# Two MLPs by one level of Strassen's algorithm: seven block products for eight

## The chip, the cores and the metric

One core of a Trainium2 chip runs the kernel. The metric is the device time of one execution in microseconds; of three runs of the kernel before the median was 3708.84 us (3703.24 to 3708.95).

TensorE multiplies: in this kernel a matmul holds a weight tile of 128x128, streams 512 columns past it and adds into a bank of 512 columns in PSUM; the part that changes uses eight banks. VectorE and ScalarE read PSUM and do everything elementwise, GpSimd works on SBUF, and SyncE (SP) issues DMAs. Each engine runs its own queue in order; they wait for each other by semaphores.

## The reference

The model works on x of 1024 tokens by 1024 channels. Two layers come first, an attention layer and a recurrent one, each followed by an MLP; then a norm and two mixed layers. All in fp32. The part that changes is the MLP:

```
def sqrelu_mlp(h, w1, w2):
    return jnp.square(jax.nn.relu(h @ w1)) @ w2
...
        x = x + sqrelu_mlp(rmsnorm(x, mlp_norm_g[layer]), mlp_w1[layer], mlp_w2[layer])
```

w1 is 1024x4096, w2 is 4096x1024. Behind the first MLP comes the recurrent layer, which starts with a norm of x; behind the second a norm and the mixed layers.

## The kernel before

All activations lie transposed: channels on partitions in eight tiles of 128, the 1024 tokens along the columns. An fp32 product is made of three: each operand is split into a high part, rounded to the fp32r that TensorE takes, and a low part, the rest, and high x high, high x low and low x high are summed.

`trunk` (L648) holds the attention's output projection (W_O), MLP 0, the recurrent layer (R_X, R_Y, R_O) and MLP 1. All weights come as panels of 128 output channels, 160 of them, through one loop on four queues:

- SP loads a panel of 512 KB into one of two slots as soon as the slot's last one was split (L151).
- GpSimd makes the high part (L711) and the low part (L713) of a panel, when TensorE is done with the slot's panel before.
- TensorE takes a panel in `product` (L198): for each of 8 chunks of input channels the three parts, for each part both halves of the tokens, so two neighbouring matmuls write two different banks (L208). 8 x 3 x 2 = 48 matmuls of 512 columns. Two panels have four banks, `pn.acc`; another four, `aux`, are for sums.
- VectorE and ScalarE empty them.

An MLP is done in four groups of 1024 hidden channels: eight panels of w1, then eight of w2. In the first kind (`mlp` of VectorE, L1002 to L1016) VectorE multiplies the relu by rstd, the norm's factor per token (L1008), ScalarE squares it (L873) and makes the high part (L875), VectorE the low part (L1011), while TensorE is at the next panel. In the second kind VectorE adds the panel to x (`add`, L977). The last panel of a group is the only one whose tile the next panel needs, as its last chunk.

Ahead of an MLP and behind it x is normed: ScalarE scales each finished tile (L859) and squares it (L861), VectorE makes the low part (L982) and sums the squares into one accumulator (L988), and TensorE sums that over the partitions (`total`, L766 to L772) before the last chunk of the next panel. ScalarE takes the root (L865), VectorE the reciprocal (L1000). Behind MLP 1 the squares are summed twice, plain and by the next norm's gain (L988, L1140).

Before the trunk's first panel TensorE runs filler matmuls (`keep_busy`, L521).

Of the kernel before, what the change touches and what calls it, by code (L numbers as in the profile page):

```python
# [2 lines left out]

# [15 lines left out]
P = 128  # L19
D = 1024  # L20
# [99 lines left out]
class Panels:  # L120
# [77 lines left out]
    def product(self, pe, u, turn, h_hi, h_lo, before_chunk=None, order=None):  # L198
# [4 lines left out]
        for k in order:  # L203
            if before_chunk:
                before_chunk(k)
            for part, (w, h) in enumerate(((self.hi, h_hi), (self.hi, h_lo), (self.lo, h_hi))):
                for s in range(2):
                    last = pe.matmul(self.acc[:, u, s * HALF:(s + 1) * HALF], w[:, u, k, :],  # L208
                                     h[:, k, s * HALF:(s + 1) * HALF],
                                     start=(k == order[0] and part == 0), stop=(k == order[-1] and part == 2))  # L210
        last.then_inc(self.sems[f"panel_done{u}"], 1)
# [272 lines left out]

class Model:
# [162 lines left out]
    def trunk(self, oT, held):  # L648
# [13 lines left out]
        with stage(nc, "tk", names) as (sems, sb, ps):  # L662
            a_lo = sb("a_lo", [P, DK, S], F32R)
            a_hi = sb("a_hi", [P, DK, S], F32R)
            with nc.sbuf_tensor("tk_xb", [P, DK, S], F32) as xb:
                pass
            b_lo = sb("b_lo", [P, DK, S], F32R)
            b_hi = sb("b_hi", [P, DK, S], F32R)
            with nc.sbuf_tensor("tk_xb_lo", [P, 2, S], F32R) as xb_lo:
                pass  # L670
            sq = sb("sq", [P, 2, S])
# [18 lines left out]
            with nc.Block() as block:  # L690
                @block.sync
                def _(sync):
                    for p in range(2, MLP[0]):
                        u = p % 2
                        sync.wait_ge(sems[f"w_split{u}"], p // 2 + 1)
                        sync.dma_start(pn.raw[:, u, W_O_AHEAD:DK, :].rearrange("p k n -> p (k n)"),
                                       self.ins["w_trunk"][p, :, W_O_AHEAD * P:]).then_inc(sems[f"w_landed{u}"], 16)
                    pn.load(sync, MLP[0] // 2)

                @block.gpsimd  # L700
                def _(pool):
# [5 lines left out]
                    def weights(turn, u, at=0):  # L707
# [4 lines left out]
                        pool.wait_ge(sems[f"w_hi{u}"], turn + 1)  # L712
                        pool.tensor_tensor(pn.lo[:, u, at:, :], pn.raw[:, u, at:, :], pn.hi[:, u, at:, :].bitcast(F32),  # L713
# [42 lines left out]
                    with pool.Fori(R_O // 2, 80) as i:  # L756
                        for u in range(2):
                            weights(i, u)

                @block.tensor  # L760
                def _(pe):
                    def ready(s):

                        return lambda k: pe.wait_ge(sems["x_lo"], DK * s + k + 1)

                    def total(s):  # L766

# [6 lines left out]
                    def first(s):  # L774

                        def before(k):
                            if k == DK - 1:
                                total(s)
                            ready(s)(k)

                        return before

                    def mlp(m, base, s):
                        hid = lambda g: (lambda k: pe.wait_ge(sems["hid_lo"], 32 * m + 8 * g + k + 1))
                        pn.product(pe, 0, base // 2, *A, first(s))
                        pn.product(pe, 1, base // 2, *A)
                        with pe.Fori(1, 4) as i:
                            for u in range(2):
                                pn.product(pe, u, base // 2 + i, *A)
                        with pe.Fori(0, 4) as i:  # L790
                            for u in range(2):
                                pn.product(pe, u, base // 2 + 4 + i, *B, hid(0))
                        with pe.Fori(1, FG) as g:
                            with pe.Fori(0, 4) as i:
                                for u in range(2):
                                    pn.product(pe, u, 8 * g + i + base // 2, *A)
                            with pe.Fori(0, 4) as i:
                                for u in range(2):
                                    pn.product(pe, u, 8 * g + i + (base // 2 + 4), *B, hid(g))
# [27 lines left out]
                    mlp(0, MLP[0], 0)  # L827
                    linear(R_X, first(1), 1)
# [2295 lines left out]
```

## Time and profile before

| | |
|---|---|
| median of 3 runs | 3708.84 us |
| the profiled execution's own time | 3708.65 us |
| its span, first to last instruction | 3706.9 us |
| granted TensorE clock, mean | 0.983 |
| TensorE busy | 3556.1 us, 96% |
| VectorE busy | 1665.9 us, 45% |
| ScalarE busy | 1096.2 us, 30% |
| GpSimd busy | 1198.2 us, 32% |

Busy time is the union of an engine's instructions; shares are of the span. In a row of the profile PE is TensorE, PEld its weight loads, DVE VectorE, ACT ScalarE and POOL GpSimd; L208 is line 208 of the kernel. The matmuls overlap in the records, so the distance of their starts is what one costs.

### The profile page before, as it was taken

The numbers are of one execution on the slowest core, as the hardware profiler recorded it, in microseconds if no ns is written. First come the engines' busy times: TensorE is split into PE (matmuls) and PEld (weight loads), VectorE is DVE, ScalarE is ACT, GpSimd is POOL, SyncE is SP. The second block draws the span as 40 slices with busy tenths as digits, with TensorE's granted clock in tenths as the row PEclk, the third lists the DMA queues.
The fourth block names the chain that finished last, engine by engine and source line by source line (L and its number), as shares of the span: only waits on it lengthen the run. The fifth ranks groups of instructions, "written<-read, shape, count | busy, mean of one in ns | idle before, by whom it ended". The sixth has DMA issues, their size and how long they took to land. (4 is left out here: it accounts for less than half of the span.)

```text
span 3706.9 us, 44331 instructions
## 1 busy us (share of the span) xinstructions
PE 3556.1 (96%) x17794; PEld 2812.5 (76%) x17794; DVE 1665.9 (45%) x1935; ACT 1096.2 (30%) x1665; POOL 1198.2 (32%) x695
## 2 busy tenths in 40 slices
PE   7999999999999999999999999899988999998898
PEld 6777777888888888788888888787645678765567
DVE  5666766312121259642121113555746542275566
ACT  2355453201010116521010101214435411253551
POOL 2455541333333337532333332222212122321214
PEclk9999999999999999999999999999999999999999
DMA  4243341111111121211111111122124121211423
GB/s 164 91 139 136 108 154 68 51 51 46 51 45 51 58 84 49 88 46 51 45 51 45 51 45 51 40 108 85 35 63 125 63 102 40 78 42 44 127 78 110
DMA packets 84159, 274.56 MB, mean 74 GB/s; under 512 B 9872, under 2 KB 11824, under 8 KB 84016
## 3 DMA queue, kind: packets, MB, share of 16 engines
q1 hardware_dynamic: 60720, 206.52, 16.3%
q10 hardware_dynamic: 16384, 40.90, 3.3%
q0 software_dynamic: 6912, 25.17, 2.0%
q8 instruction: 97, 1.59, 0.2%
q14 instruction: 46, 0.38, 0.0%
HBM read 220.39 MB, written 47.97 MB: 72 GB/s over the span
## 5 line engine op out<-in xcount | busy, mean ns | idle before, releaser
L711 POOL CAST held_hi<-held_raw 128x1024 fp32r<-128x1024 f32 (+1 forms) x158 | 174.1, 1102 | 1062.4 <-PE tk_acc L208 548.0
L208 PE MATMUL tk_acc<-tk_a_hi,held_hi 128*128 128x512 f32 x1280 | 396.4, 391 | 6.6 <-POOL held_lo L713 5.8
L208 PE MATMUL tk_acc<-tk_a_lo,held_hi 128*128 128x512 f32 x1280 | 394.7, 390 | 0.0
L208 PE MATMUL tk_acc<-tk_a_hi,held_lo 128*128 128x512 f32 x1280 | 394.6, 389 | 0.0
L873 ACT ACTIVATE tk_sq<-tk_r 128x1024 f32<-128x1024 f32 x64 | 67.9, 1061 | 1067.0 <-DVE tk_r L1008 1067.0
L713 POOL TENSOR_TENSOR held_lo<-held_raw,held_hi 128x1024 fp32r<-128x1024 f32 (+1 forms) x158 | 378.3, 2395 | 12.7
L208 PE MATMUL tk_acc<-tk_b_hi,held_hi 128*128 128x512 f32 x1200 | 369.5, 389 | 0.0
L208 PE MATMUL tk_acc<-tk_b_hi,held_lo 128*128 128x512 f32 x1200 | 369.5, 389 | 0.0
L208 PE MATMUL tk_acc<-tk_b_lo,held_hi 128*128 128x512 f32 x1200 | 369.4, 389 | 0.0
L977 DVE TENSOR_TENSOR xT<-tk_acc,xT 128x1024 f32<-128x1024 f32 x80 | 97.9, 1224 | 568.0 <-PE tk_acc L208 567.6
L208 PEld LDWEIGHTS tk_acc<-tk_a_hi,held_hi 128*128 128x128 f32 x1280 | 240.3, 188 | 58.9 <-POOL held_lo L713 7.9
L208 PEld LDWEIGHTS tk_acc<-tk_a_lo,held_hi 128*128 128x128 f32 x1280 | 240.8, 188 | 50.2
L208 PEld LDWEIGHTS tk_acc<-tk_a_hi,held_lo 128*128 128x128 f32 x1280 | 240.5, 188 | 50.1
L208 PEld LDWEIGHTS tk_acc<-tk_b_hi,held_lo 128*128 128x128 f32 x1200 | 225.2, 188 | 46.8
L208 PEld LDWEIGHTS tk_acc<-tk_b_lo,held_hi 128*128 128x128 f32 x1200 | 225.2, 188 | 46.7
L208 PEld LDWEIGHTS tk_acc<-tk_b_hi,held_hi 128*128 128x128 f32 x1200 | 225.2, 188 | 46.7
L1008 DVE SCALAR_TENSOR_TENSOR tk_r<-tk_acc,tk_rstd 128x1024 f32<-128x1024 f32 x64 | 78.4, 1224 | 393.4 <-PE tk_acc L208 393.2
L1961 PE MATMUL ma_sc<-xT 104*128 104x512 f32 (+5 forms) x384 | 157.0, 520 | 7.9 <-DMA xT<-mkpe_dram 5.2
L2513 POOL TENSOR_TENSOR da_mod_acc<-da_mod_acc,da_w_mod 128x1024 f32<-128x1024 f32 x42 | 115.6, 2753 | 124.0 <-ACT da_w_mod L2896 124.0
L2064 DVE TENSOR_REDUCE ma_st<-ma_sc 128x1 f32<-128x128 f32 (+7 forms) x128 | 96.7, 756 | 121.3 <-PE ma_sc L1961 120.6
L1011 DVE TENSOR_TENSOR tk_b_lo<-tk_sq,tk_b_hi 128x1024 fp32r<-128x1024 f32 x64 | 78.8, 1231 | 141.5 <-ACT tk_b_hi L875 141.5
L2205 ACT COPY ma_pts<-ma_pt 128x128 f32<-128x128 f32 (+7 forms) x128 | 81.7, 638 | 115.2 <-PE ma_pt L1973 114.5
(421 smaller groups left out, 6940.0 us busy)
## 6 DMA issues: line engine op xcount, KB each, us to landing
held_raw<-in_w_trunk SPq DMA_DIRECT2D x154, 512.0 KB, 3.1
da_w_mod<-in_ada_w POOLq DMA_DIRECT2D x48, 512.0 KB, 4.1
pj_w_raw<-in_w_in SPq DMA_DIRECT2D x44, 512.0 KB, 3.2
held_raw<-in_w_qkv SPq DMA_DIRECT2D x24, 512.0 KB, 3.7
ma_w_raw<-in_w_out SPq DMA_DIRECT2D x24, 512.0 KB, 3.2
x_dram<-xT ACTq DMA_DIRECT2D x16, 512.0 KB, 2.6
xT<-x_dram SPq DMA_DIRECT2D x16, 512.0 KB, 7.2
xT<-in_xT SPq DMA_DIRECT2D x13, 512.0 KB, 9.2
```

Of the source, the lines that this page charges most:

```text
L208: last = pe.matmul(self.acc[:, u, s * HALF:(s + 1) * HALF], w[:, u, k, :], h[:, k, s * HALF:(s + 1) * HALF], start=(k == order[0] and part ...
L711: pool.tensor_copy(pn.hi[:, u, at:, :], pn.raw[:, u, at:, :]).then_inc(sems[f"w_hi{u}"], 1)
L713: pool.tensor_tensor(pn.lo[:, u, at:, :], pn.raw[:, u, at:, :], pn.hi[:, u, at:, :].bitcast(F32), ALU.subtract).then_inc(sems[f"w_split{u} ...
L873: act.activation(sq[:, u, :], rr, ACT.Square).then_inc(sems["sq"], 1)
L977: dve.tensor_tensor(self.xT[:, n, :], pn.acc[:, p % 2, :], self.xT[:, n, :], ALU.add)\
L1008: dve.scalar_tensor_tensor(rr, pn.acc[:, u, :], 0.0, rstd[:, :], ALU.max, ALU.mult)\
L1011: dve.tensor_tensor(b_lo[:, n, :], sq[:, u, :], b_hi[:, n, :].bitcast(F32), ALU.subtract)\
L1961: last = pe.matmul(dst[:, part, :], q[0:rows, u % 2, m, b * P:(b + 1) * P], k[0:rows, u % 2, m, part * w:(part + 1) * w], start=True, stop ...
L2064: dve.tensor_reduce(st[:, t % 4, 1, m:m + 1], score(m, parts, w), axis=AXXY, op=ALU.max, negate=True).then_inc(sems["neg"], 1)
L2205: act.copy(pts[:, m, 0:n], pt[:, 0:n]).then_inc(sems["pts"], 1)
L2513: pool.tensor_tensor(mod_acc[:, j % 2, :], mod_acc[:, j % 2, :], w_mod[:, n % 2, :], ALU.add).then_inc(sems["mod_added"], 1)
```

## The change

A phase is a 1024x1024 block of weights times an operand of 1024 channels by 1024 tokens: four groups of an up and a down phase in each MLP, 16 in all (`ph`). Weights, operand and result are cut in two each way. Strassen's algorithm in Winograd's form makes the result's four blocks of seven products M1 to M7 of 512x512x512 blocks (before: eight), with sums of weight blocks on the left, of operand blocks on the right, and of products behind. They come in the order M1, M2, M4, M5, M6, M3, M7. A product is four units `p`, one for each tile of 128 output channels, and a unit is 12 matmuls into one bank: all four chunks high x high, then high x low, then low x high. Two units make a half-unit step `d` (14 a phase), which is the step in which weights are prepared: 128x1024 of a left operand.

- M1, M6 and M7 add up in the four banks of `pn.acc`; M2, M4, M5 and M3 in the four of `aux`. ScalarE copies M1's banks into `aux`, and M2 adds onto the copy; so each bank of `aux` is written in full by a matmul before the trunk.
- SP loads a phase's weights in eight blocks, the next phase's behind the sums that free them. GpSimd does nothing for the MLPs. ScalarE makes the high parts (`s_high`, `t_high`), VectorE the low parts (`s_low`, `t_low`) and all sums (`s_sum`, `t1_sum` to `t4_sum`), for the step or product after the one on TensorE. Weight parts have two slots by `d`, operand parts two by product.
- In an up phase VectorE relus M2's banks as it takes them, ScalarE takes M4, M5 and M6 to SBUF, VectorE adds M3 and M7 to these (two of 512 columns for each of M7's tiles), relus them (512 columns behind M3 in the last two steps, whole tiles behind M7 in the next phase's first step) and ScalarE squares them. VectorE takes all but M1 of a down phase and adds them to x.
- The panels of the other stages keep `product`; they are 32 now, and no loop is left in the MLPs. GpSimd waits for M7's units before it writes the low parts of R_X's first two panels, which share memory with the weight lows.
- Ahead of an MLP `a`, the operand in fp32, takes the place of its two parts; the sum of squares stands on TensorE behind M1's third unit; rstd's reciprocal comes in four quarters. Behind it tiles 0 to 3 of x are done with M3, tiles 4 to 7 with M7; `low_step` and `last` scale, split and square them.

The core of the diff, with twelve or more columns of indentation taken off:

```diff
+def left(d):
+    return [raw(11, d % 2), raw(12, d % 2), raw(22, d % 2), raw(22, d % 2), raw(22, d % 2), raw(22, d % 2),
+            raw(21, d % 2)][d % 14 // 2]
+def right(f, h):
+    ph, j = divmod(f, 7)
+    if j in (M1, M2, M3):
+        return operand(ph, *{M1: (0, 0), M2: (1, 0), M3: (1, 1)}[j], h)
+    if j == M6:
+        return tiles((hid_t2 if ph % 2 else a_t2)[:, h, :])
+    if j == M5 and ph % 2:
+        return tiles(t1[h])
+    return ts[:, f % 2, 1, 2 * h:2 * h + 2, :]
...
+def load_next(m):
+    for ph in range(8 * m, 8 * m + 7):
+        for at, q, d in ((12, 0, 10), (12, 1, 11), (22, 0, 10), (11, 0, 12), (22, 1, 11), (11, 1, 13),
+                         (21, 0, 12), (21, 1, 13)):
+            if at in (12, 11):
+                sync.wait_ge(sems["s_sum"], 8 * ph + d - 5)
+            else:
+                sync.wait_ge(sems["s_lo"], 14 * ph + d + 1)
+            load_block(ph + 1, at, q)
...
+    elif j == M2:
+        pe.wait_ge(sems["read_act"], wg.a_at[ph, M1, p])
...
+def product(ph, j):
+    f = 7 * ph + j
+    for p in range(4):
+        d = 2 * f + p // 2
+        if p % 2 == 0:
+            pe.wait_ge(sems["s_hi"], d + 1)
+        bank_ready(ph, j, p)
+        bank = bank_a(p) if j in (M1, M6, M7) else bank_b(p)
+        for part, (w, y) in enumerate(((s_hi, 0), (s_hi, 1), (s_lo, 0))):
+            if p % 2 == 0 and part == 2:
+                pe.wait_ge(sems["s_lo"], d + 1)
+            for k in range(4):
+                if p == 0 and k % 2 == 0 and part < 2:
+                    pe.wait_ge(sems[("t_hi", "t_lo")[part]], 2 * f + k // 2 + 1)
+                at = p % 2 * HALF + k * P
+                last = pe.matmul(bank, w[:, d % 2, at:at + P], tr[:, f % 2, y, k, :],
+                                 start=(j in (M1, M4, M5) and k == 0 and part == 0),
+                                 stop=(k == 3 and part == 2), skip_group_check=True)
+        last.then_inc(sems["unit"], 1)
+        if ph % 8 == 0 and j == M1 and p == 2:
+            total(ph // 4, 1)
...
-self.keep_busy(pe, aux[:, 1, 0:P], 28)
+self.keep_busy(pe, aux[:, 1, 0:P], 14)
+for p in range(4):
+    pe.matmul(bank_b(p), self.ident[:, :], self.xT[:, 0, 0:HALF], start=True, stop=True)
...
-mlp(0, MLP[0], 0)
-linear(R_X, first(1), 1)
+mlp(0)
+pe.wait_ge(sems["read_dve"], wg.d_at[7, M7, 1])
+linear(R_X, first_of_branch, 1)
+pe.wait_ge(sems["read_dve"], wg.d_at[7, M7, 3])
...
+    if d == 112:
+        act.wait_ge(sems["ai_done"], DK)
+    elif d >= 2:
+        act.wait_ge(sems["unit"], 2 * d - 2)
+    act.copy(tiles(s_hi[:, d % 2, :]), left(d)).then_inc(sems["s_hi"], 1)
...
+    src, dst = {M1: (bank_a(p), bank_b(p)), M4: (bank_b(p), piece(hid, p + 4, 0)),
+                M5: (bank_b(p), piece(hid, p + 4, 1)), M6: (bank_a(p), piece(hid, p, 1))}[j]
+    act.copy(dst, src).then_inc(sems["read_act"], 1)
...
+def mlp(m, finish_step):
+    for ph in range(8 * m, 8 * m + 8):
+        for d in range(14):
+            at = 14 * ph + d
+            f = at // 2
+            if not (ph % 8 == 0 and d == 0 or ph % 8 == 7 and d == 13):
+                s_high(at + 1)
+            if ph % 2 and d < 2:
+                for p in (2 * d, 2 * d + 1):
+                    square_tile(ph - 1, p)
+            if f + 1 < 56 * m + 56:
+                t_high(f + 1, d % 2)
+            prev, jj = divmod(at - 1, 14)
+            jj, q = jj // 2, (at - 1) % 2
+            if prev == ph and (jj == M1 or ph % 2 == 0 and jj in (M4, M5, M6)):
+                if ph % 8 == 0 and jj == M1 and q == 1:
+                    root(2 * m, 1)
+                    act.wait_ge(sems["root"], 2 * m + 1)
+                for p in (2 * q, 2 * q + 1):
+                    take(ph, jj, p)
...
+def park(step):
+    for kind, n in (((scaled, 0), (scaled, 1)), ((scaled, 2), (scaled, 3), (square, 0), (square, 1)),
+                    ((scaled, 4), (scaled, 5), (square, 2), (scaled, 6), (scaled, 7), (square, 3),
+                     (square, 4), (square, 5), (square, 6), (square, 7)))[step]:
+        kind(n)
...
+def s_low(d):
+    dve.wait_ge(sems["s_hi"], d + 1)
+    dve.tensor_tensor(tiles(s_lo[:, d % 2, :]), left(d), tiles(s_hi[:, d % 2, :].bitcast(F32)),
+                      ALU.subtract).then_inc(sems["s_lo"], 1)
...
+def t2_sum(ph, h):
+    hidden(ph, 1, h)
+    made(ph, f"t1_{h}")
+    difference(tiles(hid_t2[:, h, :]), operand(ph, 1, 1, h), tiles(t1[h]))
+def t4_sum(ph, h):
+    made(ph if ph % 2 else ph // 8 * 8, f"t2_{h}")
+    difference(slot(ph, M4, h), tiles((hid_t2 if ph % 2 else a_t2)[:, h, :]), operand(ph, 1, 0, h))
...
+        elif j == M7:
+            dve.tensor_tensor(x(1, 0), bank, x(1, 0), ALU.add)
+            last = dve.tensor_tensor(x(1, 1), bank, x(1, 1), ALU.add)
...
+def relu_tile(ph, p):
+    dve.wait_ge(sems["read_dve"], wg.d_at[ph, M7, p])
+    dve.scalar_tensor_tensor(hid[:, p + 4, :], hid[:, p + 4, :], 0.0, rstd[:, :], ALU.max, ALU.mult)\
+        .then_inc(sems["relu"], 1)
...
+def down(ph, finish_step):
+    end = ph % 8 == 7
+    for d in range(14):
+        at, f, h = 14 * ph + d, 7 * ph + d // 2, d % 2
+        if d == 0:
+            for p in range(2):
+                relu_tile(ph - 1, p)
+            s_low(at + 1)
+            for p in (2, 3):
+                take(ph - 1, M7, p)
+            t_low(f + 1, h)
+            for p in (2, 3):
+                relu_tile(ph - 1, p)
+            continue
+        due = [(ph, (d - 1) // 2, p) for p in ((0, 1) if d % 2 else (2, 3)) if d > 2]
+        if due:
+            take(*due[0])
+        if d == 1:
+            t1_sum(ph, 0)
+        elif d in (2, 3):
+            t2_sum(ph, h)
+        elif d in (10, 11):
+            t3_sum(ph, h)
+        if not end or d < 13:
+            s_low(at + 1)
+        if d == 1:
+            t1_sum(ph, 1)
+        elif d in (2, 3):
+            t4_sum(ph, h)
+        elif 4 <= d <= 11:
+            s_sum(at + 2)
...
+        if not end or d < 12:
+            t_low(f + 1, h)
+        if due:
+            take(*due[1])
+        if end and d >= 12:
+            finish_step(d - 12)
+    if end:
+        for p in (2, 3):
+            take(ph, M7, p)
+            finish_step(p)
...
+def low_step(step):
+    low = lambda n: split_low(n, self.col("mix_g", DK + n))
+    for kind, n in (((low, 0), (low, 1)), ((low, 2), (low, 3)), ((low, 4), (low, 5)),
+                    ((low, 6), (low, 7)) + tuple((partial(add_hidden_square, 1), n) for n in range(DK)))[step]:
+        kind(n)
...
+def last(step):
+    for n in ((0, 1), (2, 3), (4, 5), (6, 7))[step]:
+        add_hidden_square(3, n)
+        dve.wait_ge(sems["g_sq"], n + 1)
+        dve.wait_ge(sems["g_acc"], n + 1)
+        dve.tensor_tensor(rstd[:, :], rstd[:, :], a[:, n, :], ALU.add).then_inc(sems["g_acc"], 1)
```

## Rows read from the trace of the kernel before

**Rows 1.** The page's first part: busy us, share of the span, instructions.
```profile
PE 3556.1 (96%) x17794; PEld 2812.5 (76%) x17794; DVE 1665.9 (45%) x1935; ACT 1096.2 (30%) x1665; POOL 1198.2 (32%) x695
```

**Rows 2.** Windows, both MLPs: us; busy PE, PEld, DVE, ACT, POOL; clock; DMA share, GB/s.
```profile
651.00:1349.00 698.00, 698.00 (x3076) 577.29 (x3077) 155.26 (x116) 85.68 (x81) 220.96 (x128) 1.00 0.15 54
1672.00:2362.00 690.00, 690.00 (x3043) 570.68 (x3042) 148.50 (x113) 83.46 (x79) 213.22 (x124) 1.00 0.13 46
```

**Rows 3.** Timeline, VectorE amid an MLP: start, us, line, operation [idle before, releaser].
```profile
1023.05 1.23 DVE L1008 SCALAR_TENSOR_TENSOR tk_r<-tk_acc,tk_rstd 128x1024 f32<-128x1024 f32 x1 [6.21 <-PE tk_acc L208]
...
1026.49 1.23 DVE L1011 TENSOR_TENSOR tk_b_lo<-tk_sq,tk_b_hi 128x1024 fp32r<-128x1024 f32 x1 [2.21 <-ACT tk_b_hi L875]
1033.93 1.23 DVE L1008 SCALAR_TENSOR_TENSOR tk_r<-tk_acc,tk_rstd 128x1024 f32<-128x1024 f32 x1 [6.22 <-PE tk_acc L208]
```

**Rows 4.** Timeline, TensorE in the last mixed layer's output projection (two of 384).
```profile
3640.22 0.39 PE L2020 MATMUL ma_sc<-ma_hi,ma_w_hi 128*128 128x512 f32 x1
3640.44 0.39 PE L2020 MATMUL ma_sc<-ma_lo,ma_w_hi 128*128 128x512 f32 x1
```

**Rows 5.** Timeline, VectorE where its instructions follow closely.
```profile
401.89 0.67 DVE L2758 SCALAR_TENSOR_TENSOR xT<-da_x,xT 128x512 f32<-128x512 f32 x1
402.49 0.67 DVE L2759 SCALAR_TENSOR_TENSOR xT<-da_x,xT 128x512 f32<-128x512 f32 x1
...
610.46 3.50 DVE L1023 TENSOR_TENSOR tk_b_lo<-oT,tk_b_hi 128x1024 fp32r<-128x1024 f32 x3 [6.29 <-ACT tk_b_hi L880]
```

**Rows 6.** Groups by line and shape: busy us, mean ns; idle before, releasers.
```profile
L873 ACT ACTIVATE tk_sq<-tk_r 128x1024 f32<-128x1024 f32 x64 | 67.9, 1061 | 1067.0 <-DVE tk_r L1008 1067.0
...
L1636 DVE RECIPROCAL pj_rt<-pj_rt 128x256 f32<-128x256 f32 x32 | 56.1, 1753 | 17.9 <-ACT pj_rt L1484 17.1
...
L988 DVE TENSOR_TENSOR acc<-acc,tk_r 128x1024 f32<-128x1024 f32 x32 | 49.7, 1552 | 9.3 <-ACT tk_r L861 9.0
...
L2885 ACT COPY da_pts<-da_pt 128x512 f32<-128x512 f32 x48 | 28.2, 587 | 141.0 <-PE da_pt L2656 141.0
```

**Rows 7.** Timeline, VectorE at the start of the first mixed layer.
```profile
2387.25 1.28 DVE L422 SCALAR_TENSOR_TENSOR pj_ab<-xT,pj_h_g,pj_aux 128x1024 f32<-128x1024 f32 x1
2388.45 1.28 DVE L434 SCALAR_TENSOR_TENSOR m_h_lo<-pj_ab,mod,m_h_hi 128x1024 fp32r<-128x1024 f32 x1
2389.84 1.28 DVE L422 SCALAR_TENSOR_TENSOR pj_ab<-xT,pj_h_g,pj_aux 128x1024 f32<-128x1024 f32 x1
```

**Rows 8.** Timeline, the end of the first MLP.
```profile
1354.04 1.21 DVE L988 TENSOR_TENSOR acc<-acc,tk_r 128x1024 f32<-128x1024 f32 x1
...
1358.70 1.88 PE L770 MATMUL tk_aux<-acc,ones 128*128 128x512 f32 x4
```

**Rows 9.** Timeline, VectorE and GpSimd at the start of the first MLP.
```profile
652.98 2.40 POOL L713 TENSOR_TENSOR held_lo<-held_raw,held_hi 128x1024 fp32r<-128x1024 f32 x1
...
653.16 3.30 DVE L988 TENSOR_TENSOR acc<-acc,tk_r 128x1024 f32<-128x1024 f32 x1
...
657.59 1.23 DVE L988 TENSOR_TENSOR acc<-acc,tk_r 128x1024 f32<-128x1024 f32 x1
```

**Rows 10.** Windows, in the recurrent layer where TensorE stands.
```profile
1537.00:1542.00 5.00, 0.18 (x1) 0.00 (x0) 3.79 (x3) 1.06 (x1) 4.92 (x2) 1.00 0.00 0
1542.00:1545.00 3.00, 2.77 (x7) 2.21 (x8) 1.89 (x2) 1.04 (x1) 2.92 (x3) 0.58 0.52 173
```

**Rows 11.** Timeline, VectorE at the end of the second MLP.
```profile
2361.92 1.22 DVE L977 TENSOR_TENSOR xT<-tk_acc,xT 128x1024 f32<-128x1024 f32 x1 [6.17 <-PE tk_acc L208]
...
2365.41 1.22 DVE L1140 TENSOR_TENSOR tk_rstd<-tk_rstd,tk_sq 128x1024 f32<-128x1024 f32 x1
```

**Rows 12.** Timeline, TensorE at the start of the trunk.
```profile
608.38 9.19 PE L521 MATMUL tk_aux<-ones,ident 128*128 128x128 f32 x56 [3.11 <-PEq L79]
```

**Rows 13.** The page's DMA issues: count, KB each, median us to landing.
```profile
held_raw<-in_w_trunk SPq DMA_DIRECT2D x154, 512.0 KB, 3.1
```

**Rows 14.** Window in a mixed layer, columns as in rows 2.
```profile
2640.00:2710.00 70.00, 64.97 (x303) 43.54 (x303) 38.03 (x52) 24.16 (x40) 19.13 (x16) 1.00 0.07 25
```

More of the change, by code:

```diff
@@ L196, in credit, with product @@
             pe.sem_inc(self.sems[f"panel_done{u}"], 1)
-    def product(self, pe, u, turn, h_hi, h_lo, before_chunk=None, order=None):
+    def product(self, pe, u, turn, h_hi, h_lo, before_chunk=None, order=None, behind=None):
         pe.wait_ge(self.sems[f"w_split{u}"], turn + 2)
@@ L210, in product @@
                                      start=(k == order[0] and part == 0), stop=(k == order[-1] and part == 2))
+            if behind and k == behind[0]:
+                last.then_inc(self.sems[behind[1]], 1)
         last.then_inc(self.sems[f"panel_done{u}"], 1)
@@ L692, in _, with load_block @@
                 def _(sync):
[L693 to L698, printed above, removed]
+                    def load_block(ph, at, q):
+                        b, rows = at % 10 - 1, MLP[ph // 8] + 8 * (ph % 8) + 2 * q + 4 * (at // 10 - 1)
+                        sync.dma_start(raw(at, q), w_trunk[rows:rows + 2, :, b * HALF:(b + 1) * HALF]
+                                       .rearrange("a p m -> p a m")).then_inc(sems[f"raw{at}_{q}"], 16)
@@ L783, in mlp, with first_of_branch @@
[L783 to L799, printed above, removed]
+                    def first_of_branch(k):
+                        if k == DK - 1:
+                            total(1, 0)
+                        pe.wait_ge(sems["x_lo"], k + 1)
@@ L801, in blocks, with mlp @@
+                    def mlp(m):
+                        for ph in range(8 * m, 8 * m + 8):
+                            for j in range(7):
+                                product(ph, j)
                     def blocks(n):
@@ new lines, in into_mlp @@
+                    def into_mlp(m, base):
+                        for n in range(DK):
+                            if n == (6, DK - 1)[m]:
+                                if m:
+                                    s_low(112)
+                                for h in range(2):
+                                    t_low(56 * m, h)
+                            if n == DK - 1 and not m:
+                                s_low(0)
+                            add(base + n, n)
+                            if n == DK - 1:
+                                s_low(112 * m + 1)
+                            evacuated(dve, base + n)
+                            if n:
+                                add_square(2 * m, n - 1)
+                        add_square(2 * m, DK - 1)
@@ new lines, in difference, with hidden, a_t2_first @@
+                    def difference(out, x, y, op=ALU.subtract):
+                        dve.tensor_tensor(out, x, y, op).then_inc(sems["t_sum"], 1)
+                    def hidden(ph, block, h):
+                        if ph % 2:
+                            dve.wait_ge(sems["hid"], wg.squares(ph, block, h))
+                    def a_t2_first(ph, h):
+                        dve.wait_ge(sems["a_new"], ph + DK)
+                        difference(tiles(a_t2[:, h, :]), operand(ph, 1, 1, h), operand(ph, 0, 1, h))
@@ L1019, in _, with mlp @@
+                    def mlp(m, finish_step):
+                        for ph in range(8 * m, 8 * m + 8, 2):
+                            up(ph)
+                            down(ph + 1, finish_step)
                     for u in range(2):
```

414 lines of the change are left out of this document (304 added, 110 removed).

## The prediction

> **What bounds the kernel now.** I began with the page's busy times and then asked for stretches of the two MLPs. TensorE is busy 96% of the span [rows 1], and in the MLPs all of the time: 698.00 of 698 us in the first, 690.00 of 690 in the second, at granted clock 1.00, the 2.4 GHz level; VectorE works 155 and 149 us there, ScalarE 86 and 83, GpSimd 221 and 213 [rows 2]. The timeline shows the beat: VectorE's relus come every 10.88 us and each has stood 6.2 us for TensorE, never the reverse [rows 3]. A panel has 48 matmuls, so one costs 10.88 / 48 = 0.2267 us. All 128 panels of the MLPs take 1392.6 us. Only fewer matmuls, or a slower beat, can move the time here.
>
> **The change, part by part.** The sum is made against the profiled execution's own 3708.65 us (span 3706.9 and 1.75 around it), 0.2 us below the median of the three timed runs.
>
> *Removed: one panel in eight.* A phase (one 1024x1024 weight block of one MLP, 16 in all) had 8 panels of 48 matmuls; it gets 7 products of 4 units of 12, as many per product as a panel had. 16 x 10.88 = **-174.1 us**, if a matmul keeps its price. Before, neighbours alternate between two banks; now 12 in a row fill one bank, and no two share a weight tile. The output projection of the mixed layers already writes 24 in a row into one bank, with a weight tile of its own each: starts 0.22 to 0.23 us apart [rows 4]. I take no change.
>
> *Added: sums, splits and bank traffic.* I count for an up and a down phase together (28 half-units of two tiles, 28 x 5.44 = 152.3 us of TensorE). VectorE gets 28 weight lows, 28 operand lows, 16 weight sums, 14 operand sums and 4 relus of a whole tile, 90 instructions of 1024 columns; 44 bank takes and 4 relus make 48 of 512. Prices: three lows of just this form (fp32r out, behind ScalarE's cast) lie within 3.50 us [rows 5] and such a one lasts 1.23 [rows 3], so they start (3.50 - 1.23) / 2 = 1.14 apart; two of 512 start 0.60 apart [rows 5]. 90 x 1.14 + 48 x 0.60 = 131.4 us, 86% of TensorE's time: off the path on average, with little to spare. ScalarE gets 56 casts and 4 squares of 1024 at 1.06 and 28 copies and squares of 512 at 0.59 [rows 6]: 80 us, hidden. A copy from bank to bank is in no row; between 0.3 and 1.2 us a piece it stays hidden, I take 0.59, the row for PSUM to SBUF.
>
> *The start of each down phase, eight times.* Here work bunches. Time 0 is when TensorE starts the down phase's M1; M2 starts at 10.88. From about -0.3 VectorE has queued: two relus of whole tiles (1.2 each, the distance from a two-operand step of this kind to the next [rows 7]: 2.4), a weight low (1.1), the takes of M7's last two tiles (four of 512, 2.4), an operand low (1.1), two more relus (2.4): 9.2. Then t1, a weight low, t1 (3.4) and the second operand low of M2: 13.8. M2's first unit needs that low at its seventh matmul, 10.88 + 1.36 = 12.2, so TensorE stands 1.5 us. Behind it VectorE does t2, a weight low and t4 (17.2); ScalarE stands in its queue before the cast of t4 (18.2), and only behind that does it copy M1's third bank, which M2's third unit adds onto: 18.8, wanted at 10.88 + 1.5 + 5.44 = 17.8. Another 1.0. With later half-units at 3 x 1.14 + 2 x 0.60 = 4.6 us of VectorE against 5.44 the backlog is gone by the third product. Sum 2.5 us; with whole durations for the distances 4.0; below, 0. I take 3.0, nearer the rows' 1.14: 8 x 3.0 = **+24 us** (0 to 32).
>
> *The end of the first MLP.* Before, one tile was still to be added, scaled, split and squared when the last panel ended, and six chunks of the next panel hid it: the sum of squares stood on TensorE 3.4 us after its last term was ready [rows 8]. Now two of eight tiles end with the last unit (time 0), and all eight squares are summed behind the last low. VectorE from -0.6: a take 1.2, two lows 2.4, a take 1.2, two lows 2.4, then eight adds into one accumulator, each after the other, at 1.26: 16.7. The recurrent layer's first panel gets to its last chunk, before which the sum stands, at 7 x 1.36 = 9.5. So TensorE stands 7.2 us. GpSimd splits that layer's first two panels just then; beside such a split an add took 3.30 for 1.23 [rows 9], so 2 to 4 us more. After TensorE had stood 5 us the granted clock read 0.58 over the next 3 us, between its two levels [rows 10], about 1 us of work. I take **+12 us** (5 to 18). GpSimd's weight low behind the last units costs nothing, since the first panel runs 10.88 us and the low 2.40 [rows 9], nor do SP's loads of those panels, which it issues a phase ahead.
>
> *The end of the second MLP.* Before, 4.7 us from the last matmul to the end of the last add [rows 11]. Now VectorE has four adds per step (4.6 us) in the last two half-units beside its takes, so it is 3.8 us behind when the last unit ends; then take 1.2, four adds 4.6, take 1.2, four adds 4.6: 15.4. Nothing covers it. **+10.5 us** (7 to 14).
>
> *The starts of the MLPs.* The operand's eight tiles must be differenced for t2, and two quarters of rstd's reciprocal, 1.75 each [rows 6], stand in VectorE's queue before M2's takes, behind a root that ScalarE takes ahead of M1's copies: some 2 us late in the first MLP, where the output projection's panels are short, nothing in the second. **+2 us** (-2 to +5). The trunk's first panel starts behind the filler, 9.19 us for 28 matmuls [rows 12]; half of it plus four fp32 matmuls of 512 columns comes to about the same, 0 (-1 to +3).
>
> *Nothing:* loads. A phase needs eight blocks of 512 KB; one lands in 3.1 us [rows 13] and is asked for at least two half-units (10.9 us) ahead. SP's waits are in the order in which VectorE frees the blocks, and no panel load stands behind them within an MLP. GpSimd's 434 us fall away and were off the path.
>
> Sum: 3708.65 - 174.1 + 24 + 12 + 10.5 + 2 = **3583**; its own range, with the terms' ends not all at once, 3560 to 3606.
>
> **The rivals.** *VectorE becomes the bound.* If a wait shows in each instruction, the price is that of a low and the step behind it in another stage, 1.39 from start to start instead of 1.14 [rows 7]. 90 x 1.39 + 48 x 0.60 = 153.9, with the 512s dearer by as much 165.9, against 152.3: 13 to 109 us over eight pairs beside the ends' 24.5: 3572 to 3668. As a pair with VectorE full can't work off the down phase's backlog, I put it at 3606 to 3668, middle 3635. For it: 86% with in-order queues. Against it: the rows of the same form show 1.14 across a wait.
>
> *Slower: VectorE at its contended price.* The trunk's square adds average 1.55 [rows 6], because some meet GpSimd [rows 9]. At that price in the MLPs' queue, with the 512s in proportion, a pair takes 178.7 us, eight 1429, and with the ends' 24.5 the kernel 3770. It decides from 1.48 us per 1024 columns: (1392.6 - 24.5) / 8 / (90 + 48 x 0.53). Against it: GpSimd has no work in the MLPs but two panel splits at the first one's end.
>
> *The change doesn't do what it says:* TensorE pays for the new order, at 240 ns for each of 5376 matmuls +72 us, 3655; from 250 ns nothing is left. Against it the rows of one bank [rows 4].
>
> *The clock falls between units.* TensorE now meets a bank's semaphore every 12 matmuls and an operand's every few. Should it pause at many of them and its clock spend time at the 1.2 GHz level, a mean of 0.9 in the MLPs would add 1218.6 / 0.9 - 1218.6 = 135 us: 3718. In the mixed layer's 70 us with 5.0 us of idle time in pieces the granted clock stayed 1.00 [rows 14]; so little weight. The Trainium skill has this case (TensorE: Matmul & The Clock Gate, A second HAM failure mode: psum-queue depth-cycling): a kernel that goes round its banks can idle shortly between groups so often that the clock swings between its levels. By that rule 3718, by the row no change; the trace does not bear the rule out where idle pieces stay under a microsecond.
>
> **How the numbers follow.** Forecast (3560 to 3606) 0.68; below that, with no stall at the down phases, 0.05; VectorE the bound 0.16; contended 0.05; the order's price 0.03; the clock 0.03. The range runs from 3560 to 3645: 0.05 left out below, about 0.15 above. About 0.2% (7 us) is what a measurement of this kernel can tell from no change. Faster 0.91, same 0.02, slower 0.07.
>
> **What would show it.** Right: a matmul still every 0.227 us; an up phase in 7 x 10.88 = 76.2 us and a down phase in 79; TensorE idle at M2 of each down phase, released by an operand low and then by a bank copy; a stall of 7 to 12 us ahead of the recurrent layer's sum of squares. Wrong: TensorE idle in every half-unit, released by VectorE (first rival), lows of 1.5 us (second), matmuls further apart (third), a granted clock under 1 inside the MLPs (fourth). If down phases take 76 us too, the bunching was mis-sized.

## The result, and the profile after

| | before | after |
|---|---|---|
| median | 3707.36 us (3703.24 to 3708.95, four runs) | 3581.28 us (3578.77 to 3583.34, four runs) |
| the profiled execution's own time | 3708.65 us | 3583.34 us |
| its span | 3706.9 us | 3581.2 us |

The ratio is 0.9661, with a 95% interval of 0.9645 to 0.9678: 126 us faster; forecast were 3583 us.

The first part of the page and the windows of the two MLPs, which answer to [rows 1, 2]:

```profile
PE 3399.5 (95%) x17006; PEld 2668.2 (75%) x17006; DVE 2466.7 (69%) x2845; ACT 1558.7 (44%) x2241; POOL 757.0 (21%) x439
```
```profile
652.00:1274.00 622.00, 615.59 (x2690) 503.19 (x2689) 545.61 (x562) 307.57 (x361) 5.45 (x3) 1.00 0.16 52
1600.00:2223.00 623.00, 615.57 (x2691) 503.23 (x2690) 545.74 (x563) 308.75 (x362) 0.00 (x0) 1.00 0.15 48
```

TensorE is still the bound, but no longer without a gap: 6.4 and 7.4 us idle in the records of an MLP. VectorE went from 155 to 546 us, 88% of the stretch; GpSimd's work is gone but for 5 us at the end of the first. The granted clock is 1.00.

The timeline of the first down phase, around the start of M2: TensorE first, then ScalarE and VectorE.

```profile
740.28 1.07 PE L933 MATMUL tk_acc<-tk_t,held_lo 128*128 128x512 f32 x4
741.98 1.62 PE L933 MATMUL tk_aux<-tk_t,tk_s_hi 128*128 128x512 f32 x6 [0.63 <-issue]
743.75 0.73 PE L933 MATMUL tk_aux<-tk_t,tk_s_hi 128*128 128x512 f32 x2
...
747.06 1.07 PE L933 MATMUL tk_aux<-tk_t,held_lo 128*128 128x512 f32 x4
748.87 1.39 PE L933 MATMUL tk_aux<-tk_t,tk_s_hi 128*128 128x512 f32 x5 [0.75 <-ACT tk_aux L1061]
```
```profile
738.06 2.20 ACT L1072 ACTIVATE tk_xb<-tk_xb 128x1024 f32<-128x1024 f32 x2 [1.01 <-DVE tk_xb L1350]
740.34 1.05 ACT L1053 CAST tk_t<-tk_xb 128x1024 fp32r<-128x1024 f32 x1
741.30 1.05 ACT L1061 COPY tk_aux<-tk_acc 128x512 f32<-128x512 f32 x2
...
747.19 1.05 ACT L1053 CAST tk_t<-tk_ts 128x1024 fp32r<-128x1024 f32 x1 [3.85 <-DVE tk_ts L1288]
748.15 1.06 ACT L1061 COPY tk_aux<-tk_acc 128x512 f32<-128x512 f32 x2
...
742.48 1.22 DVE L1275 TENSOR_TENSOR tk_t<-tk_xb,tk_t 128x1024 fp32r<-128x1024 f32 x1
...
745.89 1.22 DVE L1288 TENSOR_TENSOR tk_ts<-held_t,tk_xb 128x1024 f32<-128x1024 f32 x1
748.28 1.22 DVE L1275 TENSOR_TENSOR tk_t<-tk_ts,tk_t 128x1024 fp32r<-128x1024 f32 x1 [1.17 <-ACT tk_t L1053]
```

M2 begins late because ScalarE's copy of M1's first bank (741.30, two of some 0.5) stands behind two squares and a cast, and the squares waited for VectorE's relus. The view says "issue" there, so this release is inferred: the copy's end fits to 0.1 us. At the seventh matmul M2 waits for its second operand low (742.48 to 743.70), and at the third unit for the copy of M1's third bank, which ScalarE reaches only after the cast of t4 (747.19), for which it stood 3.85 us. M2's first matmul comes at 741.98, 897.02, 1052.01 and 1207.04 us: 155.03 us a pair of phases, where 28 half-units take 152.3. The up phases between them take 76.16 us, without a gap, the down phases 78.87. So a down phase loses 2.7 us. The last of it comes at M4's seventh matmul.

The two ends answer to [rows 8, 10, 11]. TensorE in the kernel before: the start of the recurrent layer's first panel, its first block product, and the step from the last unit of MLP 1 by filler to the norm's sums:

```profile
1349.18 0.62 PE L208 MATMUL tk_acc<-tk_a_hi,held_hi 128*128 128x512 f32 x2
...
1395.58 0.61 PE L813 MATMUL tk_aux<-tk_b_hi,ai_hi 128*128 128x512 f32 x2
...
2361.72 4.63 PE L521 MATMUL tk_aux<-ones,ident 128*128 128x128 f32 x40
2366.77 1.47 PE L848 MATMUL tk_aux<-ones,acc 128*128 128x1 f32 x12 [0.43 <-DVE tk_rstd L1140]
```

The same places in the changed kernel, with VectorE's adds, and the clock behind the first end:

```profile
1274.24 0.61 PE L209 MATMUL tk_acc<-tk_a_hi,held_hi 128*128 128x512 f32 x2
...
1282.86 10.52 DVE L1233 TENSOR_TENSOR acc<-acc,tk_xb 128x1024 f32<-128x1024 f32 x8
...
1293.43 3.78 PE L895 MATMUL tk_aux<-acc,ones 128*128 128x512 f32 x4 [9.52 <-DVE acc L1233]
1296.23 1.60 PE L209 MATMUL tk_acc<-tk_a_hi,held_hi 128*128 128x512 f32 x2
...
1332.20 0.61 PE L957 MATMUL tk_aux<-tk_b_hi,ai_hi 128*128 128x512 f32 x2
...
2223.67 4.63 PE L569 MATMUL tk_aux<-ones,ident 128*128 128x128 f32 x40
2239.15 3.55 PE L998 MATMUL tk_aux<-ones,acc 128*128 128x1 f32 x16 [10.85 <-DVE tk_rstd L1553]
```
```profile
1293.00:1298.00 5.00, 4.57 (x8) 2.33 (x9) 0.38 (x1) 0.75 (x1) 0.00 (x0) 0.56 0.00 0
1298.00:1309.00 11.00, 11.00 (x50) 9.09 (x49) 7.20 (x8) 3.54 (x6) 5.98 (x6) 1.00 0.14 48
```

TensorE stands 9.5 us at the end of MLP 0, and the granted clock is 0.56 in the next window and 1.00 in the one behind; at the end of MLP 1 15.5 us pass from the last unit to the norm's sums, some 4.6 of them filler.

ScalarE at the start of MLP 1, ahead of the root and of M1's third copy:

```profile
1616.30 1.28 ACT L1025 ACT_TABLE_LOAD   x1
```

The root of MLP 0 has no such load ahead of it. M2's third unit stands 1.20 us in MLP 1.

### The profile page after: what moved, and what is told of

Read it like the earlier page. It is cut to its first block and busy times, and to the rows that moved or that the text cites. A ratio compares the mean times of both kernels' runs of the same rounds, so it can differ in the third digit from the quotient of the medians.

```text
span 3581.2 us, 43257 instructions
## 1 busy us (share of the span) xinstructions
PE 3399.5 (95%) x17006; PEld 2668.2 (75%) x17006; DVE 2466.7 (69%) x2845; ACT 1558.7 (44%) x2241; POOL 757.0 (21%) x439
## 5 line engine op out<-in xcount | busy, mean ns | idle before, releaser
L933 PE MATMUL tk_aux<-tk_t,tk_s_hi 128*128 128x512 f32 x2048 | 512.9, 391 | 13.8 <-ACT tk_aux L1061 7.3
L1038 ACT CAST tk_s_hi<-tk_w 128x1024 fp32r<-128x1024 f32 x224 | 235.5, 1052 | 521.0 <-PE tk_aux L933 292.5
L933 PEld LDWEIGHTS tk_aux<-tk_t,tk_s_hi 128*128 128x128 f32 x2048 | 381.3, 188 | 106.6 <-issue 19.4
L933 PE MATMUL tk_acc<-tk_t,tk_s_hi 128*128 128x512 f32 x1536 | 380.2, 390 | 0.0
L1259 DVE TENSOR_TENSOR held_lo<-tk_w,tk_s_hi 128x1024 fp32r<-128x1024 f32 x224 | 273.7, 1222 | 107.4 <-ACT tk_s_hi L1038 107.2
L933 PEld LDWEIGHTS tk_acc<-tk_t,tk_s_hi 128*128 128x128 f32 x1536 | 288.3, 188 | 60.7 <-issue 1.0
L933 PE MATMUL tk_aux<-tk_t,held_lo 128*128 128x512 f32 x1024 | 274.0, 389 | 0.0
L933 PEld LDWEIGHTS tk_aux<-tk_t,held_lo 128*128 128x128 f32 x1024 | 192.2, 188 | 40.5
L933 PE MATMUL tk_acc<-tk_t,held_lo 128*128 128x512 f32 x768 | 205.3, 389 | 0.0
L1271 DVE TENSOR_TENSOR tk_w<-tk_w 128x1024 f32<-128x1024 f32 x128 | 156.0, 1219 | 0.0
```

Source lines behind the costliest of these rows:

```text
L933: last = pe.matmul(bank, w[:, d % 2, at:at + P], tr[:, f % 2, y, k, :], start=(j in (M1, M4, M5) and k == 0 and part == 0), stop=(k == 3 a ...
L1038: act.copy(tiles(s_hi[:, d % 2, :]), left(d)).then_inc(sems["s_hi"], 1)
L1259: dve.tensor_tensor(tiles(s_lo[:, d % 2, :]), left(d), tiles(s_hi[:, d % 2, :].bitcast(F32)), ALU.subtract).then_inc(sems["s_lo"], 1)
L1271: dve.tensor_tensor(raw(out, q), raw(x, q), raw(y, q), op).then_inc(sems["s_sum"], 1)
```

## The experiments

My theory: one VectorE backlog makes the gaps of the down phases, VectorE's issue distance (1.14 and 0.60 us) says how near it is to being the bound, and its in-order queue alone sets the ends. Times are compared by their ratios to the kernel before, since each set had runs of that beside it.

**The copies alone.** Their old place, behind the cast, is left out.

```diff
+if ph % 2 and d == 2:
+    for p in (2, 3):
+        take(ph, M1, p)
 if f + 1 < 56 * m + 56:
     t_high(f + 1, d % 2)
```

> In down phases ScalarE copies M1's third and fourth bank ahead of the cast of M4's operand instead of behind it. My theory: the three gaps at M2 and the small one at M4 are one VectorE backlog that shows at whatever is wanted first. The gap of 1.14 us from start to start at M2's third unit goes, but M4's second operand low still ends at the same time, since the queue of VectorE is the same, so the gap there grows from 0.41 to about 1.4 us and the whole time stays within 2 us of the changed kernel's 3581. Rival: each gap is a wait of its own with a price of its own; the third goes with 1.0 us in each of eight down phases, 8 us in all, 3573.

3583.84 us, ratio 0.9658 (0.9645 to 0.9671): no change. TensorE's timeline of the same down phase, 1.8 us later in this run:

```profile
749.69 1.98 PE L933 MATMUL tk_aux<-tk_t,tk_s_hi 128*128 128x512 f32 x8
...
756.41 1.76 PE L933 MATMUL tk_aux<-tk_t,tk_s_hi 128*128 128x512 f32 x5 [0.67 <-ACT tk_t L1053]
```

M2's third unit starts on time (749.69), and M4 stands at its third matmul for the cast behind the same t4 sum, then 0.2 us for its low. The gap moved one product on; the rival, a price of its own for each wait, is out.

**The order of the down phase's start.** VectorE's instructions in their order, as a list and not as code (ScalarE's changes are told below):

```diff
 # d = 0
-t_low(M2, 0); relu_tile(2); relu_tile(3)
+relu_tile(2); relu_tile(3); t_low(M2, 0)
 # d = 1
-t1_sum(0); s_low; t1_sum(1); t_low(M2, 1)
+s_low; t_low(M2, 1); t1_sum(0); t1_sum(1)
 # d = 2, 3
-t2_sum(0); s_low; t4_sum(0); t_low(M4, 0); take(M2, 0); t2_sum(1); s_low; t4_sum(1); t_low(M4, 1); take(M2, 1)
+t2_sum(0); s_low; t4_sum(0); t2_sum(1); take(M2, 0); t_low(M4, 0); t4_sum(1); s_low; t_low(M4, 1); take(M2, 1)
```

> The same work in another order at the start of each down phase. ScalarE: M1's first copy ahead of the squares, the second behind the cast of M2's operand, the others ahead of M4's cast. VectorE: the relus ahead of M2's first operand low, M2's second operand low ahead of the two sums t1, and the next sum t2 and a take fill the 1.2 us in which VectorE now stands between t4 and its low. My theory (backlog): with 1.14 and 0.60 us from start to start M2's gaps all but go and M4's second operand low ends about 23.8 us after M1's start, wanted at 23.1; 0.5 to 1.3 us lost in a down phase instead of 2.6, so 10 to 17 us less than the changed kernel, 3564 to 3571. Rival: the gaps come from the number of instructions, not from their order, and then nothing is gained: within 3 us of 3581.

3565.24 us, ratio 0.9610 (0.9597 to 0.9623). The timeline at the same place, TensorE and VectorE:

```profile
740.84 1.98 PE L933 MATMUL tk_aux<-tk_t,tk_s_hi 128*128 128x512 f32 x8
...
751.72 2.69 PE L933 MATMUL tk_aux<-tk_t,tk_s_hi 128*128 128x512 f32 x8
...
747.12 1.22 DVE L1295 TENSOR_TENSOR held_t<-tk_xb,tk_r 128x1024 f32<-128x1024 f32 x1
748.26 0.68 DVE L1337 TENSOR_TENSOR xT<-tk_aux,xT 128x512 f32<-128x512 f32 x1
748.86 1.22 DVE L1282 TENSOR_TENSOR tk_t<-tk_ts,tk_t 128x1024 fp32r<-128x1024 f32 x1
```

M2 runs through (740.84 to 751.72 is 10.88), VectorE works where it stood 1.17 us before the low of t4, and what is left is 0.7 us at M4 (2.69 for 1.98). From the first unit to the last the first MLP takes 614.8 us and the second 615.7, for 622.7 and 623.7: 15.9 us less, which leaves 0.7 of the 2.7 us of a down phase. ScalarE's and VectorE's new orders ran together only, so what each is worth alone isn't shown.

**How far VectorE is from the bound.** In six up phases each weight low is preceded by one or two more of the same (shortened):

```diff
 dve.wait_ge(sems["s_hi"], d + 1)
+for i in range(n):    # n = 1, 2
+    dve.wait_ge(sems["extra"], extra[0])
+    dve.tensor_tensor(tiles(hid_t2[:, 0, :]), left(d), tiles(s_hi[:, d % 2, :].bitcast(F32)),
+                      ALU.subtract).then_inc(sems["extra"], 1)
```

> Fourteen more VectorE instructions of 1024 columns (a weight low once more, into a buffer that nothing reads) in each of six up phases, one per half-unit. My theory: an up phase has 42 instructions of 1024 columns at 1.14 us and 20 of 512 at 0.60, 59.7 of TensorE's 76.2 us, so 14 more make 75.6: just hidden, 0 to 5 us a phase, 0 to 30 in all, 3581 to 3611. Rival (VectorE at 1.39 us under load): 56 x 1.39 + 12 = 89.8, 13.6 us over TensorE's time, six times: 3663.

> Twenty-eight more VectorE instructions of 1024 columns in each of six up phases, two per half-unit. My theory: 70 x 1.14 + 12 = 91.8 us against TensorE's 76.2, so 15.6 us a phase, 93 in all, and up to 2 us more at the start of the next phase: 3675 to 3690, with TensorE waiting in every half-unit for VectorE. Rival (1.39 us under load): 70 x 1.39 + 12 = 109.3, 33 us a phase, 3780. Second rival (VectorE has more room than the starts show): under 3640.

3602.04 us, ratio 0.9704 (0.9689 to 0.9719), and 3690.94 us, ratio 0.9949 (0.9934 to 0.9965). The windows of one such up phase, with 14 more and with 28 more, and VectorE, TensorE and the clock in the second:

```profile
815.00:891.00 76.00, 75.67 (x332) 61.78 (x331) 71.98 (x72) 40.48 (x52) 0.00 (x0) 1.00 0.17 56
```
```profile
815.00:889.00 74.00, 67.02 (x281) 52.92 (x280) 72.29 (x67) 32.63 (x43) 0.00 (x0) 0.98 0.10 33
```
```profile
850.91 1.22 DVE L1260 TENSOR_TENSOR held_lo<-tk_w,tk_s_hi 128x1024 fp32r<-128x1024 f32 x1
852.05 1.22 DVE L1282 TENSOR_TENSOR tk_w<-tk_w 128x1024 f32<-128x1024 f32 x1
...
854.46 1.00 PE L933 MATMUL tk_aux<-tk_t,tk_s_hi 128*128 128x512 f32 x2 [2.52 <-DVE tk_t L1286]
```
```profile
849.00:859.00 10.00, 7.48 (x26) 5.58 (x25) 9.93 (x9) 5.72 (x9) 0.00 (x0) 0.83 0.00 0
```

With 14 TensorE still works 75.67 of 76 us and VectorE 71.98: all but hidden. Of the price, 3.8 us a phase on TensorE's path, 0.9 falls at M5 and M7 and the rest at the start of the next phase. With 28 VectorE is busy 72.29 of 74 us and TensorE waits. Instructions that follow without a wait still start 1.14 us apart (850.91, 852.05), so 1.14 holds under load; 1.39 would have given 3780. The two MLPs grew by 18.0 us a phase, 108 in all, for 93 to 105 expected. The granted clock fell there too: behind pauses of 1.63 and 2.52 us matmuls start 0.43 us apart for some microseconds, and the mean from 849 to 859 is 0.83. How much of the 18.0 us that made isn't shown.

**GpSimd beside VectorE** (shortened).

```diff
+for j in range(6):
+    pool.wait_ge(sems["t_lo"], 2 * (7 * ph + j) + 2)
+    for i in range(3):    # casts: range(4), tensor_copy(hid_t2[:, 0, :].bitcast(F32R), a[:, 0, :])
+        pool.wait_ge(sems["extra"], extra[0])
+        pool.tensor_tensor(hid_t2[:, 0, :], a[:, 0, :], a[:, 1, :], ALU.subtract).then_inc(sems["extra"], 1)
```

> GpSimd, idle in the MLPs, subtracts two tiles of 1024 columns into a buffer that nothing reads, three times in each of the first six products of six up phases, 7.2 us of a product's 10.88 at the 2.40 us of such an instruction. At the end of the first MLP of the changed kernel three lows beside 6.87 us of GpSimd's work took 1.39, 2.06 and 2.32 us for 1.27, so VectorE lost 0.29 us for each us of GpSimd. My theory goes by that: VectorE's 8.5 us a product become 10.6, just hidden: 0 to 40 us more in all, 3581 to 3620, and a VectorE mean of 1.4 to 1.6 us for the lows beside it. Rival (VectorE stands still while GpSimd works, as in the row where an add took 3.30 for 1.23): 8.5 + 7.2 = 15.7 us a product, 4.8 us over TensorE's, 36 times: 3755, slower than the kernel before.

> As in the run with GpSimd's subtractions, but with casts (one operand of 1024 columns), four in each of the same 36 products. A cast took 1.04 us alone and 2.04 beside VectorE at the end of the first MLP, where the low beside it took 2.06 for 1.27. Theory (the two engines take turns whatever GpSimd does on SBUF): VectorE loses 0.8 to 1.0 us per cast, 8.5 + 3.6 = 12.1 us a product, 1.2 over TensorE's, 36 times: 3625, lows beside it near 2 us. Rival (only GpSimd's instructions with two operands meet VectorE's): 3581 to 3590.

3709.00 us, ratio 0.9995 (0.9985 to 1.0004), and with casts 3598.97 us, ratio 0.9690 (0.9675 to 0.9705). VectorE, GpSimd and TensorE beside subtractions, and the clock behind:

```profile
839.74 0.68 DVE L1348 SCALAR_TENSOR_TENSOR tk_xb<-tk_aux,tk_rstd 128x512 f32<-128x512 f32 x1
...
842.70 3.43 DVE L1273 TENSOR_TENSOR held_lo<-tk_w,tk_s_hi 128x1024 fp32r<-128x1024 f32 x1
846.06 3.38 DVE L1285 TENSOR_TENSOR tk_w<-tk_w 128x1024 f32<-128x1024 f32 x1
849.36 1.21 DVE L1289 TENSOR_TENSOR tk_t<-tk_ts,tk_t 128x1024 fp32r<-128x1024 f32 x1
...
839.30 9.05 POOL L880 TENSOR_TENSOR held_t<-tk_a 128x1024 f32<-128x1024 f32 x3 [5.29 <-DVE tk_t L1289]
...
851.23 3.78 PE L947 MATMUL tk_aux<-tk_t,tk_s_hi 128*128 128x512 f32 x8 [3.85 <-DVE tk_xb L1348]
```
```profile
851.00:856.00 5.00, 4.77 (x12) 3.86 (x13) 4.72 (x5) 3.07 (x5) 0.20 (x1) 0.55 0.00 0
```

VectorE beside casts:

```profile
845.41 2.05 DVE L1285 TENSOR_TENSOR tk_w<-tk_w 128x1024 f32<-128x1024 f32 x1
847.39 2.05 DVE L1289 TENSOR_TENSOR tk_t<-held_raw,tk_t 128x1024 fp32r<-128x1024 f32 x1
```

My size for the subtractions fell: 3709 lies between my 3581 to 3620 and the rival's 3755. I had averaged over a stretch in which a good part of VectorE's work reads a bank. An instruction with both operands in SBUF takes 3.4 us for 1.2 beside one, the next as well, in turns, and the bank take at 839.74, while the first subtraction runs, its usual 0.68. The Trainium skill says this (SBUF — State Buffer, Who interferes with whom): two SBUF inputs on VectorE contend with a GpSimd instruction that reads SBUF, one such input doesn't; these rows agree. So each subtraction costs VectorE 2.2 us: 59.7 + 18 x 2.2 = 99.3 us a phase, 23 over TensorE's 76.2. The path grew by 21.0. A cast costs 0.84: 59.7 + 24 x 0.84 = 79.9, 3.7 over, and 2.7 came. There the mechanism held and the size was too high (7.2 a phase): I had taken 0.9 a cast and left out the slack of the seventh product, which has no casts. The subtractions ate the whole gain of the change.

**The order within a unit.**

```diff
-for part, (w, y) in enumerate(((s_hi, 0), (s_hi, 1), (s_lo, 0))):
-    for k in range(4):
+for k in range(4):
+    for part, (w, y) in enumerate(((s_hi, 0), (s_hi, 1), (s_lo, 0))):
```

> A unit takes its twelve matmuls chunk by chunk, the three parts of a chunk one after the other, as the panels do, instead of high by high of all chunks first. My theory (the order costs TensorE nothing, it only sets when a low is wanted: a weight low 0.45 us after the unit's start and not 1.81): a matmul still every 0.227 us, up phases as they are, M2's gaps up to 1 us longer in down phases: 3581 to 3590. Rival (the order has a price on TensorE, as with 240 ns for a matmul in one order): the distance changes in one direction by some ns, 5376 times, 27 us for 5 ns.

3579.31 us, ratio 0.9645 (0.9630 to 0.9660): not to be told from the changed kernel. TensorE at M2 of the same down phase, 1.3 us later in this run:

```profile
743.29 0.70 PE L933 MATMUL tk_aux<-tk_t,tk_s_hi 128*128 128x512 f32 x2 [0.63 <-issue]
...
750.19 0.70 PE L933 MATMUL tk_aux<-tk_t,tk_s_hi 128*128 128x512 f32 x2 [0.93 <-ACT tk_aux L1061]
```

A matmul still comes every 0.227 us; 5 ns more would have shown as 27 us. The MLPs take 621.4 and 622.4 us, 1.3 less each. I had expected M2's gaps to grow, and they shrank: M2 hardly waits for its operand low any more, M4 not at all in this phase, and M2's third unit stands 0.93 us instead of 0.75 for the copy.

**The end of MLP 0.** VectorE adds tiles 0 to 3, and TensorE (shortened):

```diff
+for n in range(4, DK):
+    pe.wait_ge(sems["x_sq"], DK * s + n + 1)
+    for h in range(2):
+        pe.matmul(aux[:, at, h * HALF:(h + 1) * HALF], self.ones[:, :],
+                  hid[:, n, h * HALF:(h + 1) * HALF], start=n == 4, stop=False)
 pe.wait_ge(sems["acc"], 9 * s + 9)
```

> At the end of the first MLP VectorE adds four of the eight squared tiles and TensorE sums the other four over the partitions itself, into the same bank, while it would stand. My theory (VectorE's queue alone holds the sum up: without a pause from 1264 to 1293 us): VectorE's fourth add ends 5.3 us after the last low, at 1288.2; TensorE's four sums at 1.31 us each end at 1288.6, the accumulator's at 1289.9 and not at 1297.2, and the clock stays up: 7 us less, 3574. Rival (the root and the reciprocal behind the sum, or the first branch panel's evacuation, set the pace anyway): the next wait, 1.07 us now, grows by as much, and the time stays at 3581.

3576.54 us, ratio 0.9640 (0.9627 to 0.9653): by the times alone not to be told from 0.9661. TensorE there:

```profile
1283.38 7.03 PE L896 MATMUL tk_aux<-tk_xb,ones 128*128 128x512 f32 x16
1290.25 1.88 PE L900 MATMUL tk_aux<-acc,ones 128*128 128x512 f32 x4
1291.56 1.03 PE L209 MATMUL tk_acc<-tk_a_hi,held_hi 128*128 128x512 f32 x2
```

The path from the recurrent layer's first panel to its first block product is 53.3 us for 58.0: 4.7 us less, not 7. Counted from the panel's start the accumulator's sum begins 2.8 us earlier, and behind it 1.9 us go, for the granted clock stays at 1.00 here. A tile's sum takes 1.72 us (6.87 for four); the 1.31 that I took runs only to the next start, when the last pass is still under way.

**Together.** First with a further edit: in the first phase of each MLP the root and the copies of M1's third and fourth bank stand ahead of M4's cast.

> The order of the start of the down phases (16 to 19 us gained in its own run), the split sum at the first MLP's end (7 us by my theory) and, in the first phase of each MLP, M1's third and fourth bank copied ahead of M4's cast (gaps of 0.54 and 1.59 us from start to start now, so 1.7 us): 25 us less than the changed kernel's 3581, 3556, if these are separate places on TensorE's path and one does not give back what another gains. Rival: the gain at the end of MLP 0 is given back in the recurrent layer, 3563.

3564.25 us, ratio 0.9609 (0.9596 to 0.9622), no better than the order alone and 8 us over what I expected: with that edit the MLPs took 615.2 and 617.8 us, 0.4 and 2.1 more than without. TensorE at the start of the second MLP waits for M4's cast now:

```profile
1614.34 2.70 PE L938 MATMUL tk_aux<-tk_t,tk_s_hi 128*128 128x512 f32 x6 [1.51 <-ACT tk_t L1058]
```

> The new order of the start of the down phases and the split sum at the first MLP's end together, without the change to the starts of the MLPs, whose trace showed 0.4 us more in the first MLP and 2.1 us more in the second. On TensorE's path the order took 15.9 us and the split sum 4.7 us, in places with 850 us between them at the nearest: 20 us less than the changed kernel's 3581, 3561. Rival: the split sum is given back behind the recurrent layer's first panels: 3565.

Without it: 3561.05 us (3557.53 to 3562.82), ratio 0.9593 (0.9580 to 0.9606), with MLPs of 614.8 and 615.7 us and 53.3 behind the first. It beats both kernels, the changed one by some 0.7%.

## Why the prediction was right

- *One panel in eight.* Right: between the gaps a matmul comes every 0.227 us, as it did with two banks in turn, and M2's four units take 10.88 us in the kernel with the new order. The order has no price either (the run chunk by chunk).
- *VectorE off the path on average.* Right, and the terms too: 132.8 us busy in the 155 us from 741 to 896, for 131.4 forecast. The added instructions show it under load: 1.14, not 1.39.
- *The start of each down phase.* Forecast 3.0 us (worked 2.5), measured 2.7: 22 us for 24. The mechanism, a VectorE backlog, is right, its split isn't: both forecast waits came, but with 0.3 and 0.9 us for 1.5 and 1.0. I missed the one ahead of them, 0.8 us for M1's first bank, on ScalarE behind squares that wait for the relus. Behind each wait the second matmul is some 0.1 us late too. The sum holds all the same, since later waits shrink by what an earlier one takes. I forecast the backlog gone "by the third product"; it was there, with 0.2 us.
- *The end of MLP 0.* First panel to first block product takes 58.0 us, for 46.4 before (1395.58 less 1349.18): 11.6 for the forecast 12. TensorE stood 9.5 us, for 7.2 and 2 to 4 more for GpSimd; three lows beside GpSimd took 2 us more than alone, and the eight adds 10.5 us, at 1.33 from start to start for the 1.26 that I took from no row. Behind it, with the clock at 0.56, 1.9 us went, where I had put 1.
- *The end of MLP 1.* 15.5 us to the sums, for 5.05 before: 10.4 for 10.5. The queue was as counted, 15.4: VectorE's instructions follow without a pause until the last add ends at 2239.00 us. No run tested this end alone.
- *The starts of the MLPs.* 2 us as forecast, but by luck: 0.5 came in the first, for 2, and 1.4 in the second, for 0, at M2's third unit. What I overlooked is ScalarE's table load of 1.28 us ahead of the root there (1616.30): the copy begins at 1618.74, and its bank is wanted at 1618.1. The kernel before has the load too, at 1667.22 us, but its root came 6.6 us after the load had ended. No run took the load out.
- The sum by these: 3708.65 - 174.1 + 21.7 + 11.6 + 10.4 + 2 = 3580, for 3583 in the profiled run. Most of the rest lies outside of the MLPs: the trunk's first panel starts 1.1 us later in the span than before, and what follows the norm's sums behind MLP 1 takes 2.0 us more, for a cause that isn't shown.

The rivals: VectorE becomes the bound somewhere between 14 and 28 more instructions a phase. Its contended price is real, above the 1.48 us from which it decides, but needs a GpSimd that reads SBUF in the MLPs, and that one has nothing to do there. The order has no price. In the changed kernel the clock stayed at 1.00 through the 24 gaps of the down phases, of up to 0.75 us idle, so the Trainium skill's swing by short pauses (TensorE: Matmul & The Clock Gate, A second HAM failure mode: psum-queue depth-cycling) did not come here. With VectorE or GpSimd overloaded it fell: to 0.83 behind 1.63 and 2.52 us idle in the run with 28 more instructions, and to 0.55 behind 3.85 us in the one with subtractions.

## What to carry to other kernels

When seven block products replace eight, price what the other engines take over by start-to-start distances under load, stage by stage, and look for the place where in-order queues bunch: an average of 86% says nothing of it. A gap released by one engine may be another's backlog; moving the wait alone shows which, for then it comes back one product later. Keep GpSimd off SBUF where VectorE, with two operands from SBUF, is near its limit.

## What the runs showed of the hardware

- VectorE with two SBUF operands of 1024 fp32 columns takes 3.4 us beside a GpSimd subtraction and 2.05 beside a cast, for 1.22 alone. With one operand in PSUM 512 columns take 0.68 beside a subtraction as without one.
- An fp32 sum of 1024 columns over the partitions costs TensorE 1.72 us back to back; the distance to a following fp32r matmul's start, 1.31, hides a part of it.
- Windows of 5 us show a granted clock of 0.56 after TensorE had stood 9.5 us, and 0.55 after 3.85 us in one place; a window of 10 us shows 0.83 around pauses of 1.63 and 2.52 us. With the changed kernel's pauses of up to 0.75 us in a down phase, and of 1.20 us at the start of MLP 1, it stayed at 1.00.
- A table load ahead of ScalarE's root takes 1.28 us; at the start of MLP 1 the copy for which TensorE stood 1.20 us comes right behind the two.
